# The first mixer's rounds reordered: recurrence channels alternate, scans one a round, ScalarE takes over q, k and the first taps; four modulation units move to the first FFN

## The reference

```python
mod = (silu(c) @ w_ada + b_ada).reshape(B, 9, D)          # 9 vectors m[0..8]
x = x + 0.5 * m[2] * rmsnorm(swiglu(modulate(rmsnorm(x), m[0], m[1])), g)      # FFN 1
proj = modulate(rmsnorm(x), m[3], m[4]) @ w_in                                 # the mixer
q, k, v, q_idx, k_idx, w_idx, x_lru, g_lru = split(proj)
attn = dsa_attention(q, k, v, q_idx, k_idx, w_idx, rel_bias)   # an indexer picks 64 keys a query
# the recurrence (LRU): xc = causal conv of 4 taps over x_lru
r = sigmoid(xc @ w_a + b_a); i = sigmoid(xc @ w_i + b_i)
a = exp(-8 * r * softplus(-lam)); b = sqrt(1 - a**2) * (i * xc)
h[t] = a[t] * h[t-1] + b[t];  lru = h * gelu(g_lru)
y = concat([rmsnorm(attn), rmsnorm(lru)]) @ w_out
x = x + m[5] * rmsnorm(y)
x = x + 0.5 * m[8] * rmsnorm(swiglu(modulate(rmsnorm(x), m[6], m[7])), g)      # FFN 2
```

## Time and profile before

| | us |
|---|---|
| median of 3 runs (2505.19 to 2507.14) | 2506.33 |
| the profiled execution's own time | 2506.24 |
| its span, first to last instruction | 2504.4 |
| PE busy in the span | 2420.6 (97%) |
| DVE busy / ACT busy / POOL busy | 1802.3 / 1254.9 / 381.0 |
| FFN 1 after its opening | 60 to 217 us of the span |
| mixer 1 | about 219 to 386 us |

### The profile page before, as it was taken

How to read it: one execution, slowest core, us unless ns; L and a number is a source line. 1 busy time by engine, 2 the same in 40 slices (tenths; PEclk the granted TensorE clock), 3 DMA queues, 4 the chain that set the end, 5 groups by cost and what they waited for, 6 DMA issues and landing times.

```text
span 2504.4 us, 39135 instructions
## 1 busy us (share of the span) xinstructions
PE 2420.6 (97%) x15670; PEld 2108.7 (84%) x15670; DVE 1802.3 (72%) x3442; ACT 1254.9 (50%) x1793; POOL 381.0 (15%) x310
## 2 busy tenths in 40 slices
PE   7999798999999999999999999899999999999999
PEld 7987778988888888888888887888888888888887
DVE  8787946656645778888887555754777888988555
ACT  3544545445555565555444545454565555444444
POOL 3023321002433610000000001340730000000000
PEclk9999999999999999999999999899999999999999
DMA  9696524555224454444445555324455444454554
GB/s 389 206 367 221 197 102 167 215 199 177 102 102 171 174 191 175 170 169 166 180 174 207 187 199 185 111 102 154 169 185 185 169 169 170 169 183 169 213 189 151
DMA packets 73029, 455.77 MB, mean 182 GB/s; under 512 B 9099, under 2 KB 15371, under 8 KB 20754
## 3 DMA queue, kind: packets, MB, share of 16 engines
q1 hardware_dynamic: 72162, 452.21, 50.1%
q0 software_dynamic: 688, 1.06, 0.3%
HBM read 449.17 MB, written 4.06 MB: 181 GB/s over the span
## 4 chain that ended last, share of the span: by engine, by line
PE 85%; DVE 9%; ACT 3%; POOL 1%; issue 1%; DMA 0%; SPq 0%; DVEq 0%; POOLq 0%; ACTq 0%
PE ps L379 19%; PE ps L352 16%; PE ps L353 16%; PE ps L354 16%; PE ps L381 8%; PE ps L2527 2%; DVE wlo L334 2%; PE ps L398 1%; PE ps L378 1%; DVE raw L345 1%; ACT whi L315 1%; DVE XB L1207 1%; ACT xn L475 1%; PE ps L1137 1%; PE ps L2507 1%
## 5 line engine op out<-in xcount | busy, mean ns | idle before, releaser
L315 ACT ACTIVATE whi<-raw 128x1024 fp32r<-128x1024 f32 x765 | 809.8, 1060 | 1050.7 <-PE ps L354 645.0
L334 DVE TENSOR_TENSOR wlo<-raw,whi 128x1024 fp32r<-128x1024 f32 x657 | 806.3, 1230 | 497.3 <-ACT whi L315 496.9
L379 PE MATMUL ps<-HT,whi 128*128 128x512 f32 x2048 | 718.7, 399 | 0.0
L381 PE MATMUL ps<-HT,wlo 128*128 128x256 f32 x1792 | 502.1, 280 | 0.0
L379 PEld LDWEIGHTS ps<-HT,whi 128*128 128x128 f32 x2048 | 372.3, 188 | 68.9
L352 PE MATMUL ps<-whi,CT 128*128 128x512 f32 x1024 | 404.0, 395 | 1.5 <-DVE wlo L334 1.1
L353 PE MATMUL ps<-wlo,CT 128*128 128x512 f32 x1024 | 398.7, 389 | 0.0
L354 PE MATMUL ps<-whi,CT 128*128 128x512 f32 x1024 | 398.6, 389 | 0.0
L381 PEld LDWEIGHTS ps<-HT,wlo 128*128 128x128 f32 x1792 | 338.6, 189 | 8.6
L334 POOL TENSOR_TENSOR wlo<-raw,whi 128x1024 fp32r<-128x1024 f32 x108 | 264.7, 2453 | 341.7 <-ACT whi L315 341.7
L352 PE MATMUL ps<-HT,whi 128*128 128x256 f32 x968 | 280.8, 290 | 7.5 <-DVE wlo L334 4.2
(11 more groups left out here) (393 smaller groups left out, 3317.8 us busy)
## 6 DMA issues: line engine op xcount, KB each, us to landing
raw<-in_down SPq DMA_DIRECT2D x128, 1024.0 KB, 4.9
raw<-in_up SPq DMA_DIRECT2D x128, 1024.0 KB, 4.8
raw<-in_w_in SPq DMA_DIRECT2D x41, 1024.0 KB, 4.9
raw<-in_ffn_gu SPq DMA_DIRECT2D x36, 1024.0 KB, 4.9
raw<-in_w_ada SPq DMA_DIRECT2D x28, 1024.0 KB, 6.4
raw<-in_ffn_d SPq DMA_DIRECT2D x22, 1024.0 KB, 5.9
raw<-in_w_out SPq DMA_DIRECT2D x12, 1024.0 KB, 4.9
raw<-in_w_ada SPq DMA_DIRECT2D x16, 512.0 KB, 12.9
```

Source lines behind the costliest of these rows:

```text
L315: e.activation(self.whi[:, i % NSPLIT, :], self.raw_of(i), ACT.Copy, bias=0.0, scale=1.0).then_inc(*k.inc("w_hi", ("hi", i)))
L334: e.tensor_tensor(self.wlo[:, n, :], self.raw_of(i), self.whi[:, n, :].bitcast(F32), ALU.subtract).then_inc(*k.inc("w_lo_pool" if pool els ...
L379: t = e.matmul(out.rearrange("p (a t) -> p a t", a=2), hi[:, s], self.HT[:, c, :, :], start=c == 0, stop=c == 7)
L381: t = e.matmul(out[:, 0:T], lo[:, s], self.HH[:, c, :], start=False, stop=False)
```

## The change

- Channels of the stream: `x_lru` channel c is projected in round 4 + 2c and `g_lru` channel c in 5 + 2c (before 4 + c and 8 + c); `w_in` is laid out to match.
- Index groups come one a round in rounds 5 to 10 (before two a round in 5 to 7); the eight top-k steps lie in rounds 11 to 16 (before 8 to 11).
- Gates and sigmoids of channel c in round 6 + 2c (before 7 + c); exponentials in rounds 13, 14 (two channels) and 15 (before 11 to 14); square root and GeLU in round 16 (before 15); one scan chunk a round in rounds 17 to 20, behind the heads (before two a round in 16 and 17, ahead of them); its sums in 21 and 23 (before 18 and 20).
- ACT, not DVE, writes `QT`, `KT` and the first conv tap.
- POOL keeps two `lo` of the mixer, slots 82 and 84 (before 15 of slots 71 to 99).
- Of the 36 modulation units FFN 1 carries 30 (before 26): two come early among its gate units, one more further on, and one more behind a down unit; `w_in` carries one (before 6), `w_out` one (before none), FFN 2 four at the same places.

```diff
-ON_POOL = set(range(1, 14, 2)) | set(range(71, 100, 2))
+ON_POOL = set(range(1, 14, 2)) | {82, 84}
...
+        def mixed(w, first, behind, odd=False):
             for c in range(w.shape[0]):
                 unit(w[c], "pad" if odd and c == w.shape[0] - 1 else "w")
+                if c in behind:
+                    unit(ada[first + behind.index(c)], "ada")
...
-        mixed(i["ffn1_gu"][8:], 8, 9, early=0, late=4)
-        mixed(i["ffn1_d"], 17, 9)
-        mixed(i["w_in"], 26, 6, True)
-        plain(i["w_out"])
-        mixed(i["ffn2_gu"], 32, 4)
+        mixed(i["ffn1_gu"][8:], 8, [1, 3] + list(range(4, 14)))
+        mixed(i["ffn1_d"], 20, list(range(10)))
+        mixed(i["w_in"], 30, [12], True)
+        mixed(i["w_out"], 31, [1])
+        mixed(i["ffn2_gu"], 32, [4, 9, 14, 19])
...
-        t.chans.update({4 + c: ("xr", c) for c in range(4)})
-        t.chans.update({8 + c: ("gl", c) for c in range(4)})
+        t.chans.update({4 + 2 * c: ("xr", c) for c in range(4)})
+        t.chans.update({5 + 2 * c: ("gl", c) for c in range(4)})
...
         def lru(r):
-            if 7 <= r < 11:
-                c = r - 7
+            if r in (6, 8, 10, 12):
+                c = r // 2 - 3
...
-            if 11 <= r < 15:
-                c = r - 11
+            for c in {13: (0,), 14: (1, 2), 15: (3,)}.get(r, ()):
...
-            if r == 15:
+            if r == 16:
...
+                out = {"qi": t.QI, "xr": t.XR, "gl": t.GG, "q": t.QT, "k": t.KT}[name]
+                if name == "xr":
+                    e.activation(t.XC[:, c, :], PS[:, b, 0:T], ACT.Identity, bias=self.vec("conv_b")[:, c:c + 1],
+                                 scale=self.vec("conv_w")[:, 12 + c:13 + c]).then_inc(*k.inc("act_proj", (tag, "xc", c, 3)))
...
-            if 16 <= r < 18:
-                for c in (2 * r - 32, 2 * r - 31):
+            if 17 <= r < 21:
+                c = r - 17
...
-                if name in ("q", "k"):
-                    for w in k.late(("used", i)):
-                        e.wait_ge(*w)
-                    e.tensor_scalar({"q": t.QT, "k": t.KT}[name][:, c, :], PS[:, b, 0:T], 0.125 if name == "q" else 1.0, None,
...
         for r in range(t.rounds):
             index(r)
+            attn(r)
             lru(r)
-            attn(r)
```

More of the change, by code:

```diff
@@ L1195, in head_dve, with conv_dve @@
                                 ALU.mult).then_inc(*k.inc("dve_head", (t.tag, "dg", h, tt)))
-    def conv_dve(self, e, what, need, out, src, w, b):
+    def conv_dve(self, e, what, need, out, src, w, b=None):
         k = self.k
-        for x in k.late(*need):
-            e.wait_ge(*x)
-        e.tensor_scalar(out, src, w(3), b, ALU.mult, ALU.add).then_inc(*k.inc("dve_conv", (*what, 3)))
+        if b is not None:
+            for x in k.late(*need):
+                e.wait_ge(*x)
+            e.tensor_scalar(out, src, w(3), b, ALU.mult, ALU.add).then_inc(*k.inc("dve_conv", (*what, 3)))
         for j in (2, 1, 0):
             n = 3 - j
-            for x in k.late((*what, j + 1)):
+            for x in k.late((*what, j + 1), *need):
                 e.wait_ge(*x)
@@ L1287, in index @@
                 self.free[6] = [(tag, "wx")]
[L1288 to L1295, removed]
-                            e.wait_ge(*w)
[L1297 to L1300, removed]
+            if 5 <= r < 11:
+                g = r - 5
+                tt, hs, W = t.groups[g]
+                b = 2 + g % 2
+                self.bank(e, b)
+                for j, h in enumerate(hs):
+                    q = slice(64 * (h % 2), 64 * (h % 2) + 64)
+                    for w in k.late((tag, "qi", h // 2), (tag, "ki")):
+                        e.wait_ge(*w)
+                    m = e.matmul(PS[:, b, j * W:j * W + W], t.QI[q, h // 2, tt * 128:tt * 128 + 128], t.KI[q, 0:W],
+                                 start=True, stop=True)
+                m.then_inc(*k.inc("pe_index", (tag, "index", g)))
+                self.free[b] = [(tag, "relu", g)]
         def sums_pe(what, need, src, b):
@@ L1399, in index @@
                              scale=1.0).then_inc(*k.inc("act_index", (tag, "wx")))
[L1400 to L1405, removed]
+            if 5 <= r < 11:
+                g = r - 5
+                for w in k.late((tag, "index", g), *([(tag, "scored", g - 2)] if g > 1 else [])):
+                    e.wait_ge(*w)
+                e.activation(t.RL[:, g % 2, :], PS[:, 2 + g % 2, :], ACT.Relu, bias=0.0,
+                             scale=1.0).then_inc(*k.inc("act_index", (tag, "relu", g)))
         def lru(r):
             lc = self.lc
-            if 7 <= r < 11:
-                c = r - 7
+            if r in (6, 8, 10, 12):
+                c = r // 2 - 3
                 b = 4 + c % 2
@@ L2895, in sync @@
         self.constants_sp(e)
-        self.load(e, 63)
+        self.load(e, 67)
         self.mixer1_sp(e)
@@ L3075, in lay @@
     dup = slice(ki, ki + 64)
-    pieces = [[dup, dup]] + [ch(n, c) for n in (qi, xl, gl) for c in range(4)]
+    pieces = [[dup, dup]] + [ch(qi, c) for c in range(4)] + [ch(n, c) for c in range(4) for n in (xl, gl)]
     pieces += [slice(vv, vv + 256), slice(vv + 256, vv + 512)]
```

87 lines of the change are left out of this document (39 added, 48 removed).

## The result

| | before | after |
|---|---|---|
| median of 7 runs each | 2506.44 (2505.19 to 2508.10) | 2500.40 (2496.28 to 2501.60) |
| the profiled execution, its span | 2506.24, 2504.4 | 2501.28, 2499.5 |

By the medians it is 6.0 us faster, where 12.1 were forecast. The ratio after to before is 0.9972, 95% interval 0.9960 to 0.9983, which is 7.0 us: it takes in that two of the seven executions after lie at 2496.3, the other five at 2500.2 to 2501.6. The profiled one is of the five.

What follows compares the result with a forecast made beforehand. It took the stage to be bound by PE with holes from DVE's lateness. Terms -0.3 + 4.2 + 5.7 + 1.4 - 0.6 - 1.2 + 2.1 + 0.8 = 12.1 took 2506.24 to 2494.1 us; range 2488 to 2502.5.

Steps and rivals of the forecast that it cites:

- FFN 1: End of FFN 1: the last down unit comes late, 0 to 0.5 us lost, taken as 0.3, upper bound 3.6.
- Up to round 12: Mixer up to round 12: the 2.61 wait for a `lo` and 1.6 of half clock behind it go; gain 4.2.
- Round 12 to head 0: From round 12's end to the first head: ACT's chain of 19.4 replaces the 25.1 before; gain 5.7.
- rival (a): Before head 0: ACT's chain is later, by square root's wait or longer table loads; 4 less won, 2498; chance 0.14.
- The clock behind it: Behind the first head's `KT` wait: half-clock loss falls from 3.0 to 1.6; gain 1.4, bounds 0 and 3.0.
- The heads: In the heads: later k copy costs 0.6 at head 2, modulation unit and `lo` cost 1.2 at head 7.
- The end: Mixer's end: POOL's `lo` no longer slows the second addition, PE's wait of 5.10 becomes 3.0; gain 2.1.
- The clock there: Behind the wait at the mixer's end: less PE work at half clock; gain 0.8, bounds 0 and 1.5.
- Rounds from there to the end unchanged: Sign: from PE's second wait at the mixer's end to the program's end, rounds keep their length.
- Rival (d): The hole in front of the heads merely moves behind them; gain under 5, 2503; chance 0.09.
- (b): FFN 1's end stalls PE by 3.6, or DVE's round 21/head 7 work costs 3 to 4; 2497.7; chance 0.14.
- (c): Slower: FFN 1's last down units come late one after the other, 20 lost, 12.4 won, 2514; chance 0.05.

Runs made afterwards that it cites:

- combo_pairs: Changed kernel with old unit order, 36 fill matmuls at first head, six POOL `lo` moved to DVE, index groups in pairs again; 2485.9 us, 0.9912 to before.
- fill_2: Changed kernel with 32 more unused matmuls of 256 columns on PE at the first head, ahead of its `KT` wait; 2498.5 us, 0.9965 to before.
- slot179_2: Changed kernel with the `lo` of slot 179, in layer 2's first mixer, on DVE instead of POOL; 2497.2 us, 0.9962 to before.

## Why the prediction was half right

Direction and mechanism held, and the time lies in the range; the likeliest time was 6.3 too low. By the prediction's steps, measured to S (7.4 won, forecast 12.1):

- **FFN 1**, -0.3: -0.7. The mechanism was as told: the last down unit was late and the PE waited 1.09 for its `hi`. ACT's row:

```profile
208.55 2.00 ACT L314 ACTIVATE whi<-raw 128x1024 fp32r<-128x1024 f32 x2 [3.98 <-DMA raw<-in_ffn_d]
```

  So the sign "no wait of PE in 60 to 217" did not hold, and a wait for `in_ffn_d` on the PE's path before 217, which was to show the prediction wrong, was there, at a third of the bound of 3.6. Seven executions of the same code in this stage showed 1.09, 0.69, 0.64, 0.45, 0.42 and twice none, so both numbers are inside its spread.
- **Up to round 12**, +4.2: +2.2. This is the step of the sum that failed most on the way to S. The 2.61 and its half clock did go: from the end of round 10 to that of round 11 it takes 2.8 (ACT's `hi` at 278.72 and 281.53), where before took 7.2. But the prediction costed the groups' move from two a round to one a round at nothing. Before, they take 1.71 + 1.14 + 2.30 = 5.15, after, 6.84: 1.7 lost, which combo_pairs wins back and more. The rest, 0.3, was not followed.
- **Round 12 to head 0**, +5.7: +6.2. The chain of ACT was 18.9 long where the sum had 19.4, and a table load held it 1.30, as the rows of before had it. ACT's timeline of the changed kernel:

```profile
286.62 1.06 ACT L314 ACTIVATE whi<-raw 128x1024 fp32r<-128x1024 f32 x1 [2.09 <-PE ps L353]
287.70 1.28 ACT L1421 ACT_TABLE_LOAD   x1
289.00 0.51 ACT L1421 ACTIVATE E<-R,lc 128x256 f32<-128x256 f32 x1
...
300.68 1.28 ACT L1435 ACT_TABLE_LOAD   x1
301.98 1.06 ACT L1435 ACTIVATE GG<-GG 128x1024 f32<-128x1024 f32 x1
...
305.09 0.37 ACT L1510 ACTIVATE KT<-ps 128x256 f32<-128x256 f32 x1
```

  The longer time of the Trainium skill (ScalarE: Activation LUTs, What ACT_TABLE_LOAD costs) would, as an estimate of three times 1.38, have put head 0 at 309.7; no run shows its drain. With it rival (a) falls, whose other half did not come either: ACT's square root has no wait for DVE.
- **The clock behind it**, +1.4: about -0.2. The PE had 6.5 us of work at half clock, more even than the 5.91 before and not the 3.3 of the nearest row. A wait half as long did not bring a shorter stretch. fill_2 prices it at 2.9.
- **The heads**, -1.8: -1.5 (0.75 for `KT` and 0.97 for `DG`, each at its place and near its size, less a wait of 0.26 for the sums that is gone). From head 0 to the first transpositions of the mixer's end it took 72.91 before and 74.56 after, -1.65; the clock's -0.2 is what these waits leave of it.
- **The end**, +2.1: +1.7; the wait is 2.77, forecast 3.0. **The clock there**, +0.8: -0.3. The half-clock stretch grew from 5.3 to 6.0, and the stage from there to S from 198.84 to 199.11: the step was wrong in holding that every us of PE work at half clock loses half of itself. That is so behind `KT` (2.9 won by keeping the clock), and not behind a norm (0.3).

These make 7.4. **Rounds from there to the end unchanged**, the last sentence but one of "What would show it", was the second failure: 3.7 were lost between S and D, and 1.1 won back behind D, which was not followed. That the time still fell into the range is in part the range's width: 4.7 less were won up to S than forecast, and 2.5 less behind it. Rival (d) had named a hole that moves behind the gain and its time, 2503, but put it into the heads; it lay 300 us further on. (b)'s stall of FFN 1 came at a third of its price, (c) did not come, nor (e).

What stays open: why the clock was at half for 8.8 us behind a wait of 3.69 before and for 5.6 behind the same wait after. The two executions at 2496.3 would fit the second clock drop staying away, 4.3 by slot179_2, but no profile of one was taken, so this is only argued. Why the same wait lets the clock fall in one kernel and not in the other was not found.

## What to carry to other kernels

Price a step that spreads small matmuls over more rounds by looking at which rows of the PE neighbours use: what stood side by side may have run at once. When a stage ends earlier, read the next place where the PE waits for a late engine: there the time won can turn into a longer wait, and the clock may take more than that back. And test parts of a change alone and left out: here the list of POOL's slots costs 6 us without the new rounds, and with them it wins 3.3 up to S and some 1 in the end, which is inside the noise.

## What the hardware did that was not expected

- Two groups of 64-row matmuls on the two halves of the PE's rows: 8 in 1.14 us, where 4 alone take 1.13.
- The granted clock stays at 1.00 if throwaway matmuls fill the PE's wait (at head 0 it was 0.50 without them); this won 2.9 at head 0 and 0.3 at FFN 2's start.
- Waits of 2.41 and 2.42 us in the same place, one without and one with a fall of the clock.
- Matmuls of 128 and of 256 columns cost nearly the same one behind the other, 0.117 and 0.125 us.
- DVE's three taps beside a `lo` of POOL take 3.58 instead of 1.52, and a product of two SBUF inputs 2.00 instead of 0.42. One such overlap, taken away in slot179_2, shortened the stretch from S to D by 4.3.
